# Rows of a matmul's moving operand placed at chosen distances from the weights' place in SBUF

## The reference, cut to what matters

```python
def swiglu_ffn(h, w_in, w_out):
    gate, up = jnp.split(h @ w_in, 2, axis=-1)
    return (jax.nn.silu(gate) * up) @ w_out

for layer in range(DEPTH):                      # DEPTH = 2
    h = h + 0.5 * swiglu_ffn(rms_norm(h, ffn_norm[layer, 0]), ffn_w_in[layer, 0], ffn_w_out[layer, 0])
    ...                                         # layer 0: hybrid attention mixer, layer 1: rwkv7 mixer
    h = h + 0.5 * swiglu_ffn(rms_norm(h, ffn_norm[layer, 1]), ffn_w_in[layer, 1], ffn_w_out[layer, 1])
return rms_norm(h, final_norm)[:, N_META:]
```

## Time and profile before

| | |
|---|---|
| median of 3 runs | 1876.79 us |
| the profiled execution | 1877.96 us |
| its span | 1876.2 us |
| TensorE busy | 96% of the span, 18074 matmuls |
| VectorE, ScalarE busy | 68%, 55% |
| mean granted TensorE clock | 0.989 of full |
| mean DMA rate | 148 GB/s |
| the longest chain: matmuls of L414, L415, L416 | 23%, 22%, 22% of the span |

### The profile page before, as it was taken

How to read it: one execution, slowest core, us unless ns; L and a number is a source line. 1 busy time by engine, 2 the same in 40 slices (tenths; PEclk the granted TensorE clock), 3 DMA queues, 4 the chain that set the end, 5 groups by cost and what they waited for, 6 DMA issues and landing times.

```text
span 1876.2 us, 46612 instructions
## 1 busy us (share of the span) xinstructions
PE 1808.3 (96%) x18074; PEld 1727.6 (92%) x18074; DVE 1281.0 (68%) x2615; ACT 1034.0 (55%) x2048; POOL 25.2 (1%) x20
## 2 busy tenths in 40 slices
PE   7999999999999999999999999999989988799998
PEld 7899999999998999988889999999987887699998
DVE  6688687678686665586567664666567786557754
ACT  7656656656655554546456554655455744255553
POOL 0110000110000000000000000000000000000000
PEclk9999999999999999989999999999989999999999
DMA  7455566545564655533235566555552320036663
GB/s 247 141 155 192 159 193 181 151 140 167 153 196 135 180 178 180 168 102 92 69 96 164 179 179 178 161 178 179 179 182 90 114 69 4 4 114 190 183 187 123
DMA packets 75965, 278.08 MB, mean 148 GB/s; under 512 B 8496, under 2 KB 9904, under 8 KB 75312
## 3 DMA queue, kind: packets, MB, share of 16 engines
q1 hardware_dynamic: 75824, 276.05, 48.1%
HBM read 274.96 MB, written 1.05 MB: 147 GB/s over the span
## 4 chain that ended last, share of the span: by engine, by line
PE 82%; DVE 10%; ACT 4%; issue 3%; DMA 1%; SPq 0%; DVEq 0%; ACTq 0%
PE psum L414 23%; PE psum L415 22%; PE psum L416 22%; DVE weights_low L379 3%; ACT weights_high L371 2%; PE psum L2936 1%; DMA weight_ring<-weights_in 1%; PE psum L2568 1%; PE psum L1140 1%; PE psum L725 1%; PE psum L2913 1%; PE psum L746 1%; PE psum L554 1%; PE psum L2930 1%; DVE normed L1550 1%
## 5 line engine op out<-in xcount | busy, mean ns | idle before, releaser
L379 DVE TENSOR_TENSOR weights_low<-weight_ring,weights_high 128x512 fp32r<-128x512 f32 x984 | 663.7, 693 | 435.4 <-ACT weights_high L371 424.3
L371 ACT ACTIVATE weights_high<-weight_ring 128x512 fp32r<-128x512 f32 x984 | 604.0, 628 | 533.9 <-PE psum L416 531.6
L414 PE MATMUL psum<-ffn_normed_high,weights_high 128*128 128x272 f32 x1056 | 303.9, 288 | 3.4 <-DVE weights_low L379 2.1
L416 PE MATMUL psum<-ffn_normed_high,weights_low 128*128 128x272 f32 x1056 | 302.6, 287 | 0.0
L415 PE MATMUL psum<-ffn_normed_low,weights_high 128*128 128x272 f32 x1056 | 302.6, 287 | 0.0
L414 PE MATMUL psum<-first_normed_high,weights_high 128*128 128x256 f32 x1024 | 295.8, 289 | 3.5 <-DVE weights_low L379 2.9
L415 PE MATMUL psum<-first_normed_low,weights_high 128*128 128x256 f32 x1024 | 284.8, 278 | 0.0
L416 PE MATMUL psum<-first_normed_high,weights_low 128*128 128x256 f32 x1024 | 284.8, 278 | 0.0
L414 PEld LDWEIGHTS psum<-first_normed_high,weights_high 128*128 128x128 f32 x1024 | 193.0, 188 | 14.6 <-DVE weights_low L379 7.1
L414 PEld LDWEIGHTS psum<-ffn_normed_high,weights_high 128*128 128x128 f32 x1056 | 198.9, 188 | 5.9 <-issue 5.7
L415 PEld LDWEIGHTS psum<-ffn_normed_low,weights_high 128*128 128x128 f32 x1056 | 198.9, 188 | 0.1
(11 more groups left out here) (483 smaller groups left out, 3776.2 us busy)
## 6 DMA issues: line engine op xcount, KB each, us to landing
weight_ring<-weights_in SPq DMA_DIRECT2D x507, 512.0 KB, 3.6
arena<-first_in SPq DMA_DIRECT2D x1, 2176.0 KB, 10.8
consts<-const_in SPq DMA_DIRECT2D x1, 1895.0 KB, 7.6
arena<-vec_in SPq DMA_DIRECT2D x1, 1536.0 KB, 10.5
arena<-vec_in SPq DMA_DIRECT2D x1, 1152.0 KB, 5.9
residual<-x_in SPq DMA_DIRECT2D x2, 544.0 KB, 4.9
out<-normed SPq DMA_DIRECT2D x4, 256.0 KB, 2.4
weight_ring<-weights_in SPq DMA_DIRECT2D x2, 256.0 KB, 5.1
```

The source lines that it names most:

```text
L371: nc.scalar.activation(WH[:, n % SPLIT, half], W[:, n % RING, half], ACT.Copy).then_inc(weights_high, 1)
L379: nc.vector.tensor_tensor(WL[:, n % SPLIT, half], W[:, n % RING, half], WH[:, n % SPLIT, half].bitcast(F32), ALU.subtract).then_inc(weight ...
L414: nc.tensor.matmul(psum, WH[:, s, cols], high, start=start, stop=False)
L416: return nc.tensor.matmul(psum, WL[:, s, cols], high, start=False, stop=stop)
```

## The change

Each feed-forward layer gets places of its own for its rows, moved by `FFN_SHIFT` columns, and the last layer's rows stand 256 columns apart in place of 272. `FFN_GATE` and `FFN_PROD` move by 64 columns to make room. No instruction is added, removed or reordered.

```diff
         FFN_ROW = 320
-        FFN_NORMED = [parts("ffn_normed", 13 * KC * S2, KC, FFN_ROW)] * 3 + [parts("last_normed", 13 * KC * S2, KC, S2)]
-        FFN_INNER = [parts("ffn_inner", 0, FF_CH, FFN_ROW)] * 3 + [parts("last_inner", 0, FF_CH, S2)]
-        FFN_GATE, FFN_PROD = (arena(2 * FF_CH * FFN_ROW + 2 * j * S2, 2, S2) for j in range(2))
+        FFN_SHIFT = ((16, 24), (32, 40), (48, 56), (8, 16))
+        FFN_NORMED = [parts(f"ffn_normed{use}", 13 * KC * S2 + FFN_SHIFT[use][0], KC, FFN_ROW if use < 3 else S1) for use in range(4)]
+        FFN_INNER = [parts(f"ffn_inner{use}", FFN_SHIFT[use][1], FF_CH, FFN_ROW if use < 3 else S1) for use in range(4)]
+        FFN_GATE, FFN_PROD = (arena(2 * FF_CH * FFN_ROW + 64 + 2 * j * S2, 2, S2) for j in range(2))
```

## The result

The changed kernel is slower: 1890.79 us, the median of 4 runs (1886.83 to 1892.79), beside 1876.66 us for the kernel before (4 runs, 1874.99 to 1877.51). The ratio is 1.0075, with a 95% interval of 1.0059 to 1.0091, so 11.1 to 17.1 us more. The forecast of 1878.1 and its range to 1886 missed it.

A forecast was written before the change was run, and what follows sets the result against it. The prediction took TensorE's matmul pace in the feed-forward layers as the bound. Its terms, 3.5 - 3.5 + 3.5 + 0 + 0 + 0.9 - 2.9 - 0.2, sum to +1.3 us, giving 1878.1 us, range 1869 to 1886.

The forecast's parts named there:

- The mechanism: Feed-forward layers: the row's distance from the weights sets the matmul pace, settling in whole steps of 6.67 ns.
- case D: Rival: the place has no effect, `mixer` rows differ through other work; time stays 1876.8 us; chance 0.05.
- The step that failed: All feed-forward halves: a row held at one distance settles at the step nearest to a passing row's pace.
- the term of layer 1: Layer 1, `ffn_normed` at 16: 282 ns in passing, settles at 120.0 ns, -3.5 us; bounds -3.5 and +0.7.
- The choice of L415: `mixer`: reads the second of a row's three matmuls, with same-distance neighbours: 282 ns at 16, 290 at 32, 292 at 0.
- a sign against me: Feed-forward halves: wrong on settling, not on distance, if a held pace is one no passing row of that distance comes near.
- The upper bound of layer 0: Layer 0, `ffn_normed` at 0: forecast +3.5 us, at most +5.6 with 292 - 163 = 129 ns.
- The last layer: Last layer, `ffn_normed` at 56: from 118.33 ns to 113.33 (-5.3 us) or 117.8 (-0.6), middle -2.9 us.
- Its `ffn_inner` at 0: Last layer, `ffn_inner` at 0: -2.4 to 0 us, taken as -0.2.
- The `ffn_inner` of layers 0 to 2: At 8, 24 and 40, bounded by neighbouring distances: 0, 0 and +0.9 us, within -1.8 to +1.8 or 0 to +1.8.
- C: Rival, slower: the last layer finds no quick pace; 1881.2 us, or 1885.7 with 8, 24, 40 at 126.67 ns; chance 0.30.
- B: Rival, faster: last layer at 113.33 ns, the three `ffn_inner` at 120.0; -9.6 us at most, 1867.2 us; chance 0.20.

The follow-up runs named there:

- `c1_passing`: Feed-forward rows of layers 0 to 2 pass through changing distances (288, 304 and 272 columns apart), last layer held at 40 and 24; 1885.48 us.
- `c4_normed_back`: The changed kernel with the `ffn_normed` rows of layers 0 to 2 back at distance 48; 1879.11 us, ratio 1.0022 to the kernel before.
- `b2_fine`: The changed kernel's form with all rows 320 columns apart, mostly at distances between the multiples of 8; 1880.66 us.
- `a1_swapped`: The changed kernel with its distances dealt out to other layers and the last layer held at 48; 1883.12 us, beside 1878.32 of before.
- `b1_last_48`: The kernel before with only the last layer's rows 256 columns apart, all at distance 48; 1872.09 us, ratio 0.9979.
- `d3_rest_40`: `b1_last_48` with layers 0 to 2 held at distance 40; 1869.94 us, ratio 0.9966 to the kernel before.
- `c3_last_48_again`: `b1_last_48` run once more, unchanged, for its trace; 1876.22 us.
- `d1_last_320`: `b1_last_48` with the last layer's `ffn_normed` rows 320 columns apart in place of 256; 1870.03 us, ratio 0.9975 to the kernel before.
- `d2_last_64_on`: `b1_last_48` with the last layer's `ffn_normed` rows 64 columns further on; 1867.46 us, ratio 0.9964 to the kernel before.
- `a3_apart`: The changed kernel with high and low rows at different distances from each other in every half; 1886.97 us.
- the three `a` kernels that change distances: `a1_swapped`, `a3_apart` and a third, the changed kernel with halves at 56, 16 | 24, 0 | 40, 32 | 16, 32, at 1881.67 us.
- `c2_pairs`: Feed-forward halves mostly with high and low rows 8 columns apart in distance, around 48 and 40; 1880.71 us.

## Why the prediction was wrong

**What bounds the kernel** held: TensorE's pace in the feed-forward layers, nothing else. No wait was added, VectorE and ScalarE kept their idle time, and the place of `FFN_GATE` cost nothing that the windows show.

**The mechanism** held as far as the place matters. Paces follow the distance between row and weights, as steps of 6.67 ns over a few matmuls, and they hold for a whole stretch; case D, no effect, fell with the earlier trace rows against the windows after, and so did its ground, for the edit changes places alone and no work that goes with a row's number. By the two independent read ports that the Trainium skill gives TensorE ("TensorE: Matmul & The Clock Gate", Part 2), with no bandwidth taken from the running matmul by the next weight load, there would be no difference. The traces do not agree: they show 113.33 to 120.00 ns for one shape and 123.33 to 128.89 for the other. That ScalarE and VectorE write the weights' tensors meanwhile is not what slows a row: in layer 1 of after, matmuls cost 126.68 ns while VectorE worked throughout (607 of them) and 126.67 while it was idle (224), and for ScalarE 126.70 and 126.68. That it is the weight load which meets the moving row is what is left, but it is argued and not shown.

**The step that failed** is "a row held at one distance should settle at the step nearest to what a passing row of that distance shows", and in it above all the term of layer 1: 282 ns in passing at 16, "settles at 120.0: -3.5 us". It settled at 126.67, +3.4 us, and that alone is 6.9 of the 10.4 us between the sum of +1.3 and the +11.7 measured. Its bounds of -3.5 and +0.7 didn't hold it, for they came from the same passing row. The choice of L415, "a neighbour at the same distance on both sides", looked like a clean reading and was not: `c1_passing` shows the 119.8 ns again only behind the same row as in `mixer`, with 130.0 for the matmul ahead of it. The time from start to start over a whole cycle of distances is 126.1 ns, and would have promised no gain. What I had named as a sign against me, a held pace that no passing row comes near, is what came as far as `mixer`'s order goes; behind another row, in layer 0 of `c1_passing`, a passing row at 16 does show 126.5. For 32 and for 0 the same reading came out near, at 126.67 and 125.33, the latter 1.5 us better than forecast; as the reading failed at 16, that is luck. (The upper bound of layer 0, +5.6, is +6.0 by its own figures, 1056 x (129 - 123.33).)

**The last layer** was taken at a middle, -2.9 us, between 113.33 and 117.8, the paces of distance 48. At 56 it has neither: 118.33 in after, 120.00 in `c4_normed_back`. 0.0 us was within the bounds of the term, but the middle of another distance's two paces was no estimate. Its `ffn_inner` at 0 went from 117.9 to 120.00, +0.9, outside of "-2.4 to 0": I had bounded it by passing rows again.

**The `ffn_inner` of layers 0 to 2** were at +1.1, +0.9 and 0.0 for 0, 0 and +0.9, within their bounds, in the wrong order. Bounding 8, 24 and 40 by their neighbours has no ground: `b2_fine` has 126.67 at 46, 50 and 52 around 123.33 at 44, 47 and 48.

**The rivals.** C came: the last layer found no quick pace, and that is the point from which it was to decide. Its prices of 1881.2 and 1885.7 were too low because they kept layer 1's -3.5; with +3.4 there they would have been 1888.1 and 1892.6, with the measured 1890.79 between them. B had its chance from 113.33 at distance 48, which the change doesn't use; `a1_swapped`, `b1_last_48` and `d3_rest_40` show that this pace is to be had.

Measured paces of held distances, ns, with every half of every kernel in which the high and the low rows stand alike:

| distance | 0 | 8 | 16 | 24 | 32 | 40 | 48 | 56 |
|---|---|---|---|---|---|---|---|---|
| 272 columns | 125.33 or 126.66 | 125.71 | 126.67 | 125.33 | 126.67 | 123.33 | 123.33 | 125.33 or 126.67 |
| 256 columns | 120.00 | 116.67 | 117.78 | 120.00 | 118.66 | 118.67 | 113.33 or 117.78 | 118.33 or 120.00 |

Before had the best place of these for 272 columns already. For 256 columns the change took 56 and 0, two of the worst. Most entries rest on one or two traces, and the first block shows that a place with one pace here may have a second.

**What stays open.** Why a distance has its pace, and what picks one of two. `last_normed` at 48 had 117.78 ns in the four traces with layers 0 to 2 at 48 (`b1_last_48`, `c3_last_48_again`, `d1_last_320`, `d2_last_64_on`) and 113.33 in the two with them elsewhere (`a1_swapped`, `d3_rest_40`). That speaks for a part of the layers run ahead, but doesn't show it: two of six traces would fall so by chance once in fifteen times, and the first block takes either pace in one and the same program. Several traces of `b1_last_48` and `d3_rest_40` each would tell.

## What to carry to other kernels

Where TensorE's pace is the bound, the place of the moving rows against the weights, modulo 64 columns, was worth 3 to 6% of a stretch here: measure each distance held, in the stage that is to have it, before giving it one. Don't read a held pace from single matmuls of rows that pass through distances; time whole cycles from start to start, as a short matmul may stand behind a long one. Keep shapes apart when you compare a page's mean durations, since a renamed tensor can bring another shape into the group. And judge an edit of some us by the paces of its own stretches, since the rest of such a program varies by as much, partly because its stretches may take either of two paces in each execution anew.

## What the runs showed that I had not expected

- Of two matmul streams with equal shapes, one ran at 123.33 and one at 128.89 ns, through the place of the high and low rows alone (before and `a3_apart`), at a granted clock of 1.00.
- A single column changes the pace: 126.67 ns at distance 46, 123.34 at 47 (`b2_fine`).
- One placement can have two paces, 113.33 and 117.78 ns, or 118.33 and 120.00. A stretch of 934 matmuls keeps one to its end, and the next stretch, behind a stop, may have the other.
- The choice can differ between two executions of one program: 113.4 and 117.8 ns in the same 394 matmuls of the first block (`b1_last_48` and its repetition). The long stretches of the feed-forward layers repeated in all three pairs of traces.
- Settled paces are often whole steps of 6.67 ns over one to three matmuls, in 36 of the 50 halves of after, the three `a` kernels that change distances, `b2_fine`, `c2_pairs` and the last layer of `c1_passing`: 124.44 is 56 steps in three, 128.89 is 58, 116.67 is 35 in two. Paces such as 125.33, 125.71 and 118.33 are not.
